# Hyena's transforms over even and odd tokens, rotations on GpSimd, and one filler quarter moved ahead of the attention loop

## The reference, cut to what matters

```python
def fftconv(u, hk, dbias):                       # 256 tokens, 512 channels
    y = irfft(rfft(u, n=2 * L, axis=1) * hk, n=2 * L, axis=1)[:, :L]
    return y + u * dbias

z = parts[0]                                     # proj[..., :1536] after a convolution over 3 tokens
for n in range(2):
    z = parts[n + 1] * fftconv(z, hk[:, n], dbias[n])

q = rope_2d(proj[..., 1536:2048], row, col)      # 4 heads, two halves of 64 each
k = concatenate([rope_2d(proj[..., 2048:2560], row, col), k_ctx])
a = softmax(q1 k1 / 8) - lam * softmax(q2 k2 / 8)
o = a @ v                                        # then a norm of each head
gates = sigmoid(proj[..., 3072:])                # 2048 columns
```

## Time and profile before

| | |
|---|---|
| time, median of 3 runs | 1320.81 us (1318.42 to 1324.71) |
| the profiled execution | 1318.56 us, of which the span of its instructions is 1316.8 us |
| PE busy | 1278.4 us, 97% of the span |
| DVE, ACT, GpSimd (POOL) busy | 695.5 us, 500.4 us, 77.8 us |
| granted TensorE clock | 0.999 of full speed |

### The profile page before, as it was taken

One profiled execution on the slowest core, in us unless ns is written; L12 is line 12 of the kernel. 1 busy time (PEld: TensorE's weight loads), 2 busy tenths in 40 slices (PEclk: granted clock), 3 DMA queues, 4 the chain that ended last, 5 costly groups with the idle time before them and its releaser, 6 DMA issues.

```text
span 1316.8 us, 17834 instructions
## 1 busy us (share of the span) xinstructions
PE 1278.4 (97%) x7078; PEld 892.6 (68%) x7078; DVE 695.5 (53%) x1192; ACT 500.4 (38%) x766; POOL 77.8 (6%) x86
## 2 busy tenths in 40 slices
PE   8999999999999999999999999999999999999998
PEld 7987886976675454444444444449957687799986
DVE  5675678667564322223222222257875877755552
ACT  5556574345332111111111111146414685744442
POOL 5740200100000000000000000000000000000000
PEclk9999999999999999999999999999999999999999
DMA  9654747959855999999999999995505235655540
GB/s 351 232 189 151 240 144 286 353 186 333 312 203 217 401 429 428 427 429 426 428 428 428 428 427 427 426 389 185 179 13 210 110 137 159 194 165 180 190 160 33
DMA packets 102100, 363.15 MB, mean 276 GB/s; under 512 B 4114, under 2 KB 28949, under 8 KB 89920
## 3 DMA queue, kind: packets, MB, share of 16 engines
q1 hardware_dynamic: 98656, 352.86, 69.1%
q0 software_dynamic: 3168, 9.06, 2.1%
q10 hardware_dynamic: 192, 0.06, 0.0%
HBM read 360.91 MB, written 1.05 MB: 275 GB/s over the span
## 4 chain that ended last, share of the span: by engine, by line
PE 86%; DVE 6%; ACT 4%; issue 2%; DMA 1%; ACTq 0%; DVEq 0%
PE bank L532 38%; PE bank L925 16%; PE bank L943 8%; PE bank L902 5%; PE bank L1290 5%; PE bank L972 3%; DVE ring_parts L1338 2%; PE bank L854 1%; PE bank L933 1%; PE bank L1093 1%; PE bank L1082 1%; ACT ring_parts L2163 1%; PE bank L586 1%; DMA ring<-in_w_xkv 1%; PE bank L621 1%
## 5 line engine op out<-in xcount | busy, mean ns | idle before, releaser
L2163 ACT ACTIVATE ring_parts<-ring 128x1024 fp32r<-128x1024 f32 x234 | 242.6, 1057 | 226.5 <-PE bank L532 198.7
L1338 DVE TENSOR_TENSOR ring_parts<-ring,ring_parts 128x1024 fp32r<-128x1024 f32 x214 | 257.0, 1223 | 129.8 <-ACT ring_parts L2163 126.9
L532 PE MATMUL bank<-ring_parts,arena_parts 128*128 128x512 f32 x1056 | 271.8, 392 | 3.6 <-ACT ring_parts L2163 1.5
L532 PEld LDWEIGHTS bank<-ring_parts,arena_parts 128*128 128x128 f32 x1056 | 196.5, 188 | 48.7 <-ACT ring_parts L2163 2.9
L532 PE MATMUL bank<-arena_parts,ring_parts 128*128 128x256 f32 x1504 | 198.0, 284 | 2.2 <-DVE ring_parts L1338 1.2
L925 PE MATMUL bank<-ring,arena 128*64 128x512 f32 x432 | 190.6, 594 | 9.1 <-issue 9.1
L926 PE MATMUL bank<-ring,arena 128*64 128x512 f32 x448 | 198.0, 595 | 0.0
L532 PEld LDWEIGHTS bank<-arena_parts,ring_parts 128*128 128x128 f32 x1504 | 190.1, 192 | 4.1 <-issue 2.7
L925 PEld LDWEIGHTS bank<-ring,arena 128*64 128x64 f32 x432 | 57.4, 137 | 127.6 <-issue 127.6
L532 PE MATMUL bank<-ring_parts 128*128 128x512 f32 (+1 forms) x624 | 117.1, 345 | 2.1 <-DVE ring_parts L1338 1.2
L532 PEld LDWEIGHTS bank<-ring_parts 128*128 128x128 f32 x624 | 96.6, 190 | 22.0 <-issue 7.1
(11 more groups left out here) (390 smaller groups left out, 1416.2 us busy)
## 6 DMA issues: line engine op xcount, KB each, us to landing
ring<-in_w SPq DMA_DIRECT2D x81, 2048.0 KB, 21.5
ring<-in_w_in SPq DMA_DIRECT2D x27, 2048.0 KB, 9.6
flank<-in_w SPq DMA_DIRECT2D x13, 2048.0 KB, 22.1
ring<-in_w_ada SPq DMA_DIRECT2D x12, 2048.0 KB, 8.7
ring<-in_w_ffn_gate SPq DMA_DIRECT2D x11, 1024.0 KB, 5.4
ring<-in_w_ffn_up SPq DMA_DIRECT2D x11, 1024.0 KB, 8.0
ring<-in_w_ffn_down SPq DMA_DIRECT2D x5, 2048.0 KB, 7.7
ring<-in_w_xkv SPq DMA_DIRECT2D x4, 2048.0 KB, 16.4
```

Source lines behind the costliest of these rows:

```text
L532: mm = pe.matmul(ps[:, o:o + width], *pair, start=(o == 0 and kk == 0 and ha + hw == 0), stop=(kk == kn - 1 and (ha, hw) == terms[-1] and ...
L1338: dve.tensor_tensor(low, src, high, ALU.subtract).then_inc(low_ready, 1)
L2163: act.activation(high, src, ACT.Copy).then_inc(high_ready, 1)
```

## The change

Tokens are taken by parity: the tiles are now the even and the odd tokens, where they were the first and the last 128. An even token's cosine at frequency f equals that at the mirrored frequency up to a sign, so 128 frequencies are computed, and sums and differences of the even and the odd part give the other 128. Each transform has half the products on PE; ACT copies the even parts out of PSUM (`even_halves`), and DVE does the sums and differences. The spectra are done in the same way (`spectra_of_halves` on DVE, within the experts' steps 2 and 3). The tables of the way back are the first half of the old ones. `rotate` moves to POOL, word for word. Fillers move: all of p3 stands behind the first transform, none between the first way back and the second transform, and from p6.3 on each filler is one place earlier, with p7.0 ahead of the attention loop. DVE makes one more low part ahead of the loop; ACT's high parts stay where they were.

```diff
@@ tensor engine
-                for t in range(NT):
-                    mm = pe.matmul(ps[:], tab[:, t, f * P:(f + 1) * P], hF[:, t, ...], start=(t == 0), stop=(t == 1))
-                give(f"spec{o}{part}{f}", mm)
+                give(f"spec{o}{part}{f}", pe.matmul(ps[:], tab[:, f, 0:P], hF[:, f, ...], start=True, stop=True))
...
-                        mm = pe.transpose(ps[:, j * P:(j + 1) * P], uT[:, 4 * i + j, t * P:(t + 1) * P], ident[:])
+                        mm = pe.transpose(ps[:, j * P:(j + 1) * P], uT[:, 4 * i + j, t:N:2], ident[:])
...
+                for parity in range(2):
+                    if o:
+                        pe.wait_ge(s["Z_ready"], parity + 1)
+                    else:
+                        emptied(pe, f"utok{parity}0")
+                    for part in range(2):
+                        ps = bank(f"U{o}{part}{parity}")
+                        give(f"U{o}{part}{parity}", pe.matmul(ps[:], tabs[part][:, parity, 0:P], (Z if o else UT)[:, parity, 0:DHY],
+                                                              start=True, stop=True))
...
+                for parity in range(2):
+                    pe.wait_ge(s["Y_ready"], 2 * o + parity + 1)
+                    ps = bank(f"conv{o}{parity}")
+                    for part, Y in enumerate((Yre, Yother)):
+                        mm = pe.matmul(ps[:], tabs[part][:, 0, parity:N:2], Y[:, parity, :], start=(part == 0), stop=(part == 1))
+                    give(f"conv{o}{parity}", mm)
...
-            filler("p3", 0, 1)
             transformed(0)
-            filler("p3", 2, 3)
+            filler("p3", 0, 1, 2, 3)
             convolved(0)
-            filler("p5", 0)
             transformed(1)
-            filler("p5", 1, 2, 3)
+            filler("p5", 0, 1, 2, 3)
             convolved(1)
...
-            filler("p6", 2)
+            filler("p6", 2, 3)
...
-            filler("p6", 3)
+            filler("p7", 0)
...
-                filler(("p7", "p8")[n // 4], n % 4)
+                filler(("p7", "p8", "p9")[(n + 1) // 4], (n + 1) % 4)
...
-            filler("p9", 0)
+            filler("p9", 1)
             attended(H * NT - 1)
-            filler("p9", 1, 2, 3)
+            filler("p9", 2, 3)
@@ vector engine
+            def spectra_of_halves(o):
...
+                even, odd = spectra[:, 0, o], spectra[:, 1, o]
+                did(dve.tensor_tensor(even, even, odd, ALU.add))
+                did(dve.scalar_tensor_tensor(out=odd, in0=odd, scalar=-2.0, in1=even, op0=ALU.mult, op1=ALU.add))
...
-            rotate(Kall)
             split_low(2)
...
+                for part, X in enumerate((Yre, Yim)):
+                    emptied(dve, f"U{o}{part}0")
+                    odd = full(dve, f"U{o}{part}1")
+                    did(dve.tensor_tensor(X[:, 0, :], evens[:, part, :], odd[:], ALU.add), hold=False)
+                    did(dve.tensor_tensor(X[:, 1, :], evens[:, part, :], odd[:], ALU.subtract), free(f"U{o}{part}1"))
+                did(dve.tensor_tensor(Ytmp, Yre, hr, ALU.mult), hold=False)
+                did(dve.tensor_tensor(Yother, Yim, hi, ALU.mult))
+                did(dve.tensor_tensor(Ytmp, Ytmp, Yother, ALU.subtract))
+                did(dve.tensor_tensor(Yother, Yre, hi, ALU.mult))
+                did(dve.tensor_tensor(Yim, Yim, hr, ALU.mult), hold=False)
+                did(dve.tensor_tensor(Yre[:, 0, :], Ytmp[:, 0, :], Ytmp[:, 1, :], ALU.add), hold=False)
+                did(dve.tensor_tensor(Yre[:, 1, :], Ytmp[:, 0, :], Ytmp[:, 1, :], ALU.subtract))
+                did(dve.tensor_tensor(Yim, Yim, Yother, ALU.add))
+                did(dve.tensor_tensor(Yother[:, 0, :], Yim[:, 0, :], Yim[:, 1, :], ALU.add), s["Y_ready"])
+                did(dve.tensor_tensor(Yother[:, 1, :], Yim[:, 0, :], Yim[:, 1, :], ALU.subtract), s["Y_ready"])
...
+            for o in range(2):
+                filtered(o)
                 for t in range(NT):
+                    split_low(1)
+                    gated_on(o, t)
+                if o == 0:
+                    split_low(2)
             split_low(1)
...
-            split_low(2)
+            split_low(3)
@@ scalar engine
+            def even_halves(o):
+                for part in range(2):
+                    ps = full(act, f"U{o}{part}0")
+                    did(act.activation(evens[:, part, :], ps[:], ACT.Copy), free(f"U{o}{part}0"), hold=False)
+
+            even_halves(0)
+            split_high(2)
             for t in range(NT):
                 for i in (1, 2):
                     ps = full(act, f"utok{t}{i}")
...
-            split_high(6)
+            split_high(4)
             evicted("p3", Q)
+            even_halves(1)
             split_high(4)
             evicted("p5", Vall)
...
-                if n % 4 == 3:
+                if n % 4 == 2:
                     gate_columns(1 + n // 4)
@@ GpSimd, at the end of its program
+            pool.wait_ge(s["rope_in"], 32)
+            emptied(pool, "p4_0", "p4_1")
+            rotate(Kall)
+            emptied(pool, "p3_0", "p3_1")
+            rotate(Q)
```

More of the change, by code:

```diff
@@ L271, in two_blocks @@
         Z = tiles(3072, NT, DHY)
+        evens, Yother = [actT[:].rearrange("p k n -> p (k n)")[:, D * i:D * (i + 1)].rearrange("p (i n) -> p i n", i=2) for i in range(2)]
         bias_row = arena[0:1, 8192:9216]
@@ L1072, in transformed @@
             def transformed(o):
-                fcos, fsin = unit("dftB", 2, N, 0), unit("dftB", 2, N, 512)
-                if o:
-                    pe.wait_ge(s["Z_ready"], 2)
-                else:
-                    emptied(pe, "utok00", "utok10")
-                for part, tab in enumerate((fcos, fsin)):
-                    for f in range(2):
-                        ps = bank(f"U{o}{part}{f}")
-                        for t in range(NT):
-                            mm = pe.matmul(ps[:], tab[:, t, f * P:(f + 1) * P], (Z if o else UT)[:, t, 0:DHY], start=(t == 0), stop=(t == 1))
-                        give(f"U{o}{part}{f}", mm)
@@ L1085, in convolved @@
-            def convolved(o):
-                icos, isin = unit("dftB", 2, N, 1024), unit("dftB", 2, N, 1536)
-                pe.wait_ge(s["Y_ready"], 4 * (o + 1))
-                for t in range(NT):
-                    ps = bank(f"conv{o}{t}")
-                    n = 0
-                    for tab, Y in ((icos, Yre), (isin, Yim)):
-                        for f in range(2):
-                            mm = pe.matmul(ps[:], tab[:, f, t * P:(t + 1) * P], Y[:, f, :], start=(n == 0), stop=(n == 3))
-                            n += 1
-                    give(f"conv{o}{t}", mm)
+                tabs = unit("dftB", 2, N, 0), unit("dftB", 2, N, 512)
@@ L1858, in step @@
                 low(n, 1)
+                if n in (2, 3):
+                    spectra_of_halves(n - 2)
                 if not before:
@@ L1960, in gated_on @@
-            def gated_on(o):
-                for t in range(NT):
-                    emptied(dve, f"utok{t}{o + 1}")
-                    ps = full(dve, f"conv{o}{t}")
-                    did(dve.tensor_tensor(Z[:, t, :], ps[:], UT[:, t, (o + 1) * 512:(o + 2) * 512], ALU.mult), free(f"conv{o}{t}"))
-                    dve.sem_inc(s["Z_ready"], 1)
-            filtered(0)
-            split_low(1)
-            gated_on(0)
-            split_low(3)
-            emptied(dve, "p3_0", "p3_1")
-            rotate(Q)
@@ L1973, in _ @@
-            filtered(1)
-            split_low(2)
-            gated_on(1)
+                for part, X in enumerate((Yre, Yim)):
[4 more added lines that the diff above has]
+                did(dve.tensor_tensor(Ytmp, Yre, hr, ALU.mult), hold=False)
@@ new lines, in filtered, with gated_on @@
+                did(dve.tensor_tensor(Yother[:, 0, :], Yim[:, 0, :], Yim[:, 1, :], ALU.add), s["Y_ready"])
+                did(dve.tensor_tensor(Yother[:, 1, :], Yim[:, 0, :], Yim[:, 1, :], ALU.subtract), s["Y_ready"])
+            def gated_on(o, t):
+                emptied(dve, f"utok{t}{o + 1}")
+                ps = full(dve, f"conv{o}{t}")
+                did(dve.tensor_tensor(Z[:, t, :], ps[:], UT[:, t, (o + 1) * 512:(o + 2) * 512], ALU.mult), free(f"conv{o}{t}"))
+                dve.sem_inc(s["Z_ready"], 1)
@@ L2729, in _, with rotate @@
             pool.dma_start(rows[:, 3, :], w["g_ffn_post_2"].broadcast_to([P, D])).then_inc(s["rowsh_in"], 16)
+            def rotate(v, tiles_of=range(NT)):
+                for t in tiles_of:
+                    a = v[:, t, :].rearrange("p (c d) -> p c d", d=64)
+                    b = work[:, 0:512].rearrange("p (c d) -> p c d", d=64)
+                    a4 = v[:, t, :].rearrange("p (c r h d) -> p (c r) h d", r=2, h=2, d=16)
+                    b4 = work[:, 0:512].rearrange("p (c r h d) -> p (c r) h d", r=2, h=2, d=16)
+                    for hf in range(2):
+                        for r in range(2):
```

(6 more changed lines are left out.)

48 lines of the change are left out of this document (13 added, 35 removed).

## The result

The changed kernel takes 1342.12 us (1341.4 to 1342.93) against 1321.1 for the kernel before: a ratio of 1.0157, with an interval of 1.0132 to 1.0183. It is 21 us slower, where 9 were forecast (1330) and 1341 was the upper end. The direction was right, and most terms came out near their sizes; in the profiled executions 11.5 of the 23.1 us were in no term.

What follows compares the result with a forecast made beforehand. PE was taken to bound the convolutions, and weight loads the experts. Terms -12.9 + 3.0 + 0.9 + 5.3 + 3.4 + 14.2 - 2.3 = +11.6 on the profiled 1318.56 gave 1330 us, range 1315 to 1341.

Steps and rivals of the forecast that it cites:

- the one on the spectra: Halved spectra ahead of the experts bring SP's first expert load forward, lasting to the end: -2.3 us (-0.9 to -3.6).
- The terms of the convolutions: Halved products -12.9, start of the first transform +3.0, first way back +0.9, second way back +5.3.
- the first way back: Convolutions: DVE's chain just fits behind four filler quarters; one long POOL rotation instruction makes PE wait +0.9 us.
- +5.3: Second way back: PE waits for DVE's chain, at least 1.1, plus 4.2 for turns with POOL; bounds 1.1 and 9.5.
- The loop: Attention loop: DVE's low part behind ACT's high part of the same step closes a ring of 7.2 us: +14.2.
- The filler ahead of the loop: p7.0 ahead of the attention loop waits for ACT's gate copies behind the keys' copies: +3.4 us.
- The start: First transform: PE's fourth product and first filler wait for ACT to empty banks, so fillers start later: +3.0 us.
- The port: Second way back: DVE's instructions with two SBUF inputs take turns with POOL's rotation: 4.2 us.
- no turns on the port: Rival: DVE loses nothing to POOL in the convolutions; 4.9 us less, 1325.3; chance 0.17.
- the 1311: Rival case: attention loop stays paced by PE, and no turns on the port; the other side's chance is 0.15 altogether.
- 1306: Rival "faster still": loop paced by PE, no turns on the port, also no wait at the start; chance 0.05.
- Products removed: Convolutions: two transforms and two ways back keep half of 6.46 us each on PE: -12.9 us.

Runs made afterwards that it cites:

- both shifts: Changed kernel with PE's program 32 places back by more idle transposes: 1335.33 us; kernel before with its program 32 places forward: 1327.47 us.
- the run on the start: Changed kernel with ACT's four copies of the transposes and two high parts ahead of its copies of the even parts: 1338.59 us.
- theory A's edit in the loop's run: Changed kernel with ACT's high parts one quarter further ahead in the attention loop: 1329.5 us.
- the last version: Changed kernel with all repairs, earlier high parts, gate copies ahead of the loop's high parts, and POOL's rotation of the keys taken apart: 1311.12 us, 0.9935.

## Why the prediction was wrong

**The step that failed** is the one on the spectra: "this lasts to the end: -2.3". It priced the products taken out there as PE's time alone, in two ways. SP's first load for the experts was to come as much earlier; it came 0.14 earlier, since PE's saving went into a wait of 2.61 for DVE and a slower clock behind it. That the experts ended 1.8 us earlier all the same is luck as far as the runs show. And PE's program stood in the sum at nothing: taking the products out moved the code behind the experts' branch, and PE stood 5.8 us there and ran 2.2 us slower up to the transposes, 7.9 of the 11.5 that were missed. Shown by both shifts, +7.6 on the kernel before and -6.8 on the changed one. No rival held this, since the rows of before show no gap there, and the rule on fetched blocks was not weighed.

**Waits priced at their length alone.** The terms of the convolutions came to -3.7, and -2.1 was measured, although no single wait was longer than forecast: 0 for +0.9 (the first way back), 4.93 for +5.3. The difference is half speed: the four pairs of L1090 take 5.6 (998.97 to 1004.61) where half of the old group is 3.23, and the first fillers 12.5 (963.49 to 976.00) where 11.6 was assumed; the run on the start, with no wait ahead of them, has 11.49. In the loop two fillers at half speed (steps 1 and 3) cost PE 3.1, but the ring set the step, so little of it shows.

**What held.** The loop: +14.2 forecast, +14.8 measured, the step 7.2 to 7.3, and theory A's edit in the loop's run undid 12.6 of it; most of the rest is gate copies. The filler ahead of the loop: 3.4 forecast, 3.18 measured, undone in full. The start: 3.0 forecast; PE waited 2.21, and the fillers began 5.8 behind the end of the transposes (957.69 to 963.49, with the end at start and length of the row), 2.6 more than the halved transform takes. Undone, it gave 2.1 in the stretch (954.70 to 1002.55, 47.9, against 50.0), because DVE's chain was waited for instead. The port: 4.2 forecast, and 3.6 less wait (4.93 to 1.33) without it. The Trainium skill ("SBUF — State Buffer", section "SBUF: two separate sides") says that a GpSimd instruction that reads SBUF and a DVE instruction with two SBUF inputs lock each other out of a shared port for a whole instruction; the trace agrees, with 2.32 and 2.20 beside POOL and 1.22 without it.

**Sums of rivals.** Two don't follow from the terms, and the miss doesn't hang on them: no turns on the port takes off 4.2 and 0.9, 5.1 and not 4.9, and without the start's 3.0 the 1311 becomes 1308 and not 1306.

**Products removed.** -12.9 was right. In the last version no clock falls in the four groups, and they hold PE for 3.03, 3.51, 3.04 and 3.12 us (from 949.58, 965.42, 968.93 and 984.79 to the next row), 12.7 where 4 x 6.46 = 25.8 stood: -13.1. This version gains 9 us over the kernel before and not 13, since it still waits 1.32, 1.33 and 2.06 where the kernel before doesn't, with a slower clock behind the 2.06. The strided loads cost little: the 24 transposes take 3.03 where 2.78 stood.

**What stays open:** the +0.8 behind the loop, the 1.7 within the experts' loop, why the clock falls behind one wait and not behind another of the same length, and how far ahead of a branch PE's program has to be fetched. Only two positions, 32 places apart, were tried.

## What to carry to other kernels

A product that is taken out also moves the program behind it: where a branch lies ahead, look for a gap of PE with no releaser and for the instruction queue's blocks, and shift the code before the change is blamed. When a loop's high part and low part come from two engines, count in which step each writes the quarter that the other needs; one call more on one side alone closed a ring of 7.3 us here. And work that goes to GpSimd isn't free for DVE: place it where DVE idles or reads PSUM (DVE's sums from PSUM took 0.68 us beside GpSimd and without it), with cover for its whole length, and price each wait of PE with the halved clock that can come behind it.

## What was not expected of the hardware

PE's fetch of its own program cost 5.81 and 5.86 us behind the branch, in two kernels with other data and the same position, and nothing at 32 instructions' distance. Behind many waits of PE the granted clock went to half for some microseconds (0.54 and 0.55 above), so that the wait of 4.93 cost 2.4 more (5.6 for the four pairs of L1090 where 3.23 was due). It doesn't go by the wait's length: in the changed kernel the filler behind 1.84 lasts 4.57 and those behind 1.88 and 2.96 last 3.0, and behind the same 3.18 ahead of the loop the filler lasts 3.00 there and 4.58 in the run that held the queries' rotation back. Behind the waits of 1.1 to 1.4 in the convolutions and the loop of these runs it did not fall.
